# Three rounded-operand products in place of each float32 product in the second mixer of a two-layer kernel

## The reference

```python
proj = jnp.einsum('bsd,df->bsf', h, w_in)
q_a, k_a, v_a, z_a, q_r, k_r, v_r, z_r = jnp.split(proj, IN_SPLIT_IDX, axis=-1)
# 8 heads of 128: scores q_a k_a^T with three dilated windows and a slope for distance, softmax, times v_a
y_a = dilated_attention_mixture(q_a, k_a, v_a)
# 4 retention heads: (q_r k_r^T * decay) v_r in both directions, q_r and k_r of 128, v_r of 256, then a norm
y_r = bidirectional_retention(q_r, k_r, v_r, dec_f, dec_b)
y = jnp.concatenate([y_a * jax.nn.silu(z_a), y_r * jax.nn.silu(z_r)], axis=-1)
out = jnp.einsum('bsf,fd->bsd', y, w_out)
```

## Time and profile before

| | |
|---|---|
| time of the runs | 1528.95 us median of 3 (1528.47 to 1529.10) |
| time of the profiled execution | 1529.12 us |
| its span between first and last instruction | 1527.5 us |
| granted PE clock, mean | 0.998 |
| PE busy | 1513.2 us, 99% |
| DVE busy | 1138.6 us, 75% |
| ACT busy | 780.2 us, 51% |

### The profile page before, as it was taken

How to read it: one execution, slowest core, us unless ns; L and a number is a source line. 1 busy time by engine, 2 the same in 40 slices (tenths; PEclk the granted TensorE clock), 3 DMA queues, 4 the chain that set the end, 5 groups by cost and what they waited for, 6 DMA issues and landing times. The chain is left out here.

```text
span 1527.5 us, 32035 instructions
## 1 busy us (share of the span) xinstructions
PE 1513.2 (99%) x12546; PEld 1475.2 (97%) x12546; DVE 1138.6 (75%) x1389; ACT 780.2 (51%) x936; POOL 35.8 (2%) x61
## 2 busy tenths in 40 slices
PE   9999999999999999999999999999999999999997
PEld 8999997999999999999999999999999989999997
DVE  7878777668998878788788887879874644764754
ACT  7645456545454444444444444445654644454544
POOL 0000000000000000000000000000100000000000
PEclk9999999999999999999999999999999999999999
DMA  9574556557887867677676776866475554445451
GB/s 343 179 274 161 201 195 204 194 176 262 306 300 237 294 230 275 247 248 275 236 286 236 259 274 220 302 220 220 159 255 193 194 193 161 159 163 179 163 182 56
DMA packets 86428, 340.29 MB, mean 223 GB/s; under 512 B 9784, under 2 KB 10320, under 8 KB 79824
## 3 DMA queue, kind: packets, MB, share of 16 engines
q1 hardware_dynamic: 77904, 281.05, 53.1%
q0 software_dynamic: 7584, 55.61, 10.4%
q10 hardware_dynamic: 864, 2.53, 0.5%
HBM read 337.02 MB, written 2.13 MB: 222 GB/s over the span
## 5 line engine op out<-in xcount | busy, mean ns | idle before, releaser
L742 DVE TENSOR_TENSOR wlo<-raw,whi 128x1024 fp32r<-128x1024 f32 x528 | 642.6, 1222 | 332.2 <-ACT whi L359 328.4
L359 ACT ACTIVATE whi<-raw 128x1024 fp32r<-128x1024 f32 x527 | 556.6, 1060 | 631.8 <-PE PS L1421 561.8
L1417 PE MATMUL PS<-gh,whi 128*128 128x256 f32 x3048 | 846.1, 278 | 1.2 <-DVE wlo L742 0.9
L1421 PE MATMUL PS<-gh,wlo 128*128 128x256 f32 x3048 | 839.2, 275 | 0.0
L1419 PE MATMUL PS<-gl,whi 128*128 128x256 f32 x3048 | 839.1, 275 | 0.0
L1417 PEld LDWEIGHTS PS<-gh,whi 128*128 128x128 f32 x3048 | 572.2, 188 | 6.0 <-DVE wlo L742 2.7
L1419 PEld LDWEIGHTS PS<-gl,whi 128*128 128x128 f32 x3048 | 572.3, 188 | 0.8
L1421 PEld LDWEIGHTS PS<-gh,wlo 128*128 128x128 f32 x3048 | 572.1, 188 | 0.0
L1417 PE MATMUL PS<-ah,whi 128*128 128x256 f32 x688 | 189.2, 275 | 0.0
L1421 PE MATMUL PS<-ah,wlo 128*128 128x256 f32 x688 | 189.2, 275 | 0.0
L1419 PE MATMUL PS<-al,whi 128*128 128x256 f32 x688 | 189.2, 275 | 0.0
(11 more groups left out here) (272 smaller groups left out, 939.6 us busy)
## 6 DMA issues: line engine op xcount, KB each, us to landing
raw<-weights SPq DMA_DIRECT2D x527, 512.0 KB, 3.8
ada_w<-w_ada POOLq DMA_DIRECT2D x48, 1024.0 KB, 6.9
EM<-rows POOLq DMA_DIRECT2D x1, 3072.0 KB, 13.4
X<-xT SPq DMA_DIRECT2D x3, 512.0 KB, 8.7
c<-const ACTq DMA_DIRECT2D x1, 1536.0 KB, 6.9
c_act<-c_rows POOLq DMA_DIRECT2D x1, 1024.0 KB, 6.7
KF<-rows POOLq DMA_DIRECT2D x2, 512.0 KB, 6.1
outT<-X SPq DMA_DIRECT2D x2, 512.0 KB, 3.2
```

The lines of the kernel that those rows point to most:

```text
L359: act.activation(whi[:, j % SPLIT, first:first + 1024], raw[:, j, :], ACT.Copy).then_inc(s_hi, 1)
L742: dve.tensor_tensor(wlo[:, j % SPLIT, first:first + 1024], raw[:, j, :], whi[:, j % SPLIT, first:first + 1024].bitcast(F32), ALU.subtract) ...
L1417: pe.matmul(out[:, t, :], whi[:, b, w], hi[:, kt, :], start=first and half == 0 and (apart or t % 2 == 0), stop=False, skip_group_check=True)
L1421: mm = pe.matmul(out[:, t, :], wlo[:, b, w], hi[:, kt, :], start=False, stop=last and half == 1, skip_group_check=True)
```

## The change

Queries, keys, values, probabilities and decayed retention scores of the second mixer also get a high and a low part, and each of their float32 matmuls becomes three matmuls on `fp32r` parts (`split_product`). The low parts lie in tiles of `QB` that are idle at that time (table `LOW`), `QBR` being the same memory seen as `fp32r`.

The tiles:

```diff
+        QBR, _ = place("QBR", [P, 56, S], F32R, offset=ada_at)
+        LOW = {QR2: V02, KR2: V12, VR2: Q12, VR2 + 4: K12, Q02: QR2, K02: KR2, V02: VR2, Q12: Q02, K12: K02, V12: V02}
+        PTH2, _ = place("PTH2", [P, 2, 2, S], F32R, offset=o_pts)
+        PTL2 = QBR[:, VR2 + 4:VR2 + 8, :].rearrange("p (h c) s -> p h c s", h=2)
+        RETH, RETL = QBR[:, K02:K02 + 2, :], QBR[:, K02 + 2:K02 + 4, :]
```

ACT, in attention step 4, in retention step 0 and at the end of a group:

```diff
-                        act.activation(PTS[:, h % 2, :, :], PS[:, 5, :].rearrange("p (c d) -> p c d", c=2),
-                                       ACT.Copy).then_inc(s_pts, 1)
+                        act.activation(PTH2[:, h % 2, :, :], PS[:, 5, :].rearrange("p (c d) -> p c d", c=2),
+                                       ACT.Copy).then_inc(s_pth, 1)
...
+                    if step == 0:
+                        act.wait_ge(s_rs, r + 1)
+                        if r:
+                            act.wait_ge(s_ro, r)
+                        act.activation(RETH, SB2[:, r % 2, :, :], ACT.Copy).then_inc(s_rh, 1)
...
-                    act.activation(QB[:, 4 * g:4 * g + 4, :], acc_tiles((G_IN2 + g) % 2), ACT.Copy).then_inc(s_evac, 1)
+                    if 4 * g in LOW:
+                        act.activation(QBR[:, 4 * g:4 * g + 4, :], acc_tiles((G_IN2 + g) % 2), ACT.Copy).then_inc(s_qh, 1)
+                    else:
+                        act.activation(QB[:, 4 * g:4 * g + 4, :], acc_tiles((G_IN2 + g) % 2), ACT.Copy).then_inc(s_evac, 1)
```

DVE, in attention step 4, in `decayed` and two new functions, and where they are called in the slots:

```diff
+                if step == 4 and layer:
+                    dve.wait_ge(s_pth, h + 1)
+                    dve.tensor_tensor(PTL2[:, h % 2, :, :], PS[:, 5, :].rearrange("p (c d) -> p c d", c=2),
+                                      PTH2[:, h % 2, :, :].bitcast(F32), ALU.subtract).then_inc(s_pts, 1)
...
-                                         SCALE, DM[:, r, :, :], ALU.mult, ALU.mult).then_inc(s_rm, 1)
+                                         SCALE, DM[:, r, :, :], ALU.mult, ALU.mult).then_inc(s_rs, 1)
+
+            def decayed_low(r):
+
+                dve.wait_ge(s_rh, r + 1)
+                dve.tensor_tensor(RETL, SB2[:, r % 2, :, :], RETH.bitcast(F32), ALU.subtract).then_inc(s_rm, 1)
+
+            def low_part(g):
+
+                dve.wait_ge(s_qh, g - 3)
+                low = LOW[4 * g]
+                dve.tensor_tensor(QBR[:, low:low + 4, :], acc_tiles((G_IN2 + g) % 2),
+                                  QBR[:, 4 * g:4 * g + 4, :].bitcast(F32), ALU.subtract).then_inc(s_evac, 1)
...
+                    if step == 1:
+                        decayed_low(r)
...
+                if n % 8 == 7 and 4 * (n // 8) in LOW:
+                    low_part(n // 8)
                 slot2(n)
```

PE:

```diff
+            def split_product(out, left, left_low, right, right_low, first, last):
+
+                pe.matmul(out, left, right, start=first, stop=False, skip_group_check=True)
+                pe.matmul(out, left, right_low, start=False, stop=False, skip_group_check=True)
+                return pe.matmul(out, left_low, right, start=False, stop=last, skip_group_check=True)
...
-                            mm = pe.matmul(PS[:, 5, S * c:S * c + S], QB[:, KR2 + r, P * c:P * c + P], QB[:, QR2 + r, :],
-                                           start=True, stop=True)
+                            mm = split_product(PS[:, 5, S * c:S * c + S], *(QBR[:, k + r, P * c:P * c + P] for k in (KR2, LOW[KR2])),
+                                               *(QBR[:, k + r, :] for k in (QR2, LOW[QR2])), True, True)
...
-                                mm = pe.matmul(PS[:, 6, S * e:S * e + S], v,
-                                               SB2[:, r % 2, c, :], start=(c == 0), stop=(c == 1))
+                                mm = split_product(PS[:, 6, S * e:S * e + S], v, v_low, RETH[:, c, :], RETL[:, c, :], c == 0,
+                                                   c == 1)
```

More of the change, by code:

```diff
@@ L180, in build @@
         SB2, o = place("SB2", [P, 2, 2, S], offset=o)
+        o_pts = o
         PTS2, o = place("PTS2", [P, 2, 2, S], offset=o)
@@ L276, in build @@
         s_early, s_early_hi = sem("s_early"), sem("s_early_hi")
+        s_qh, s_pth, s_rs, s_rh = sem("s_qh"), sem("s_pth"), sem("s_rs"), sem("s_rh")
         s_copy, s_pool = sem("s_copy"), sem("s_pool")
@@ L1604, in attention @@
                 if layer:
-                    q, k = (QB[:, head_tile(*at_, h), :] for at_ in ((Q02, Q12), (K02, K12)))
-                    v = values(QB, V02 if h < 4 else V12, P)
+                    q, k = (tuple(QBR[:, tile + h % 4, :] for tile in (at_, LOW[at_]))
+                            for at_ in ((Q02, K02) if h < 4 else (Q12, K12)))
+                    v = tuple(values(QBR, tile, P) for tile in ((V02, LOW[V02]) if h < 4 else (V12, LOW[V12])))
                 else:
@@ L1638, in scores @@
                     at, keys = (S * c, S) if layer else (P * c, P + P * c)
-                    mm = pe.matmul(PS[:, 4, at:at + keys], q[:, P * c:P * c + P], k[:, 0:keys], start=True, stop=True)
+                    if layer:
+                        mm = split_product(PS[:, 4, at:at + keys], *(x[:, P * c:P * c + P] for x in q), *k, True, True)
+                    else:
+                        mm = pe.matmul(PS[:, 4, at:at + keys], q[:, P * c:P * c + P], k[:, 0:keys], start=True, stop=True)
                     if c == 1:
@@ L1659, in weighted @@
                     first = 0 if layer else P * b
-                    mm = pe.matmul(PS[:, 6, first:S], v(b, P * (h % 4)), PTS[:, h % 2, b, 0:S - first],
-                                   start=(b == 1), stop=(b == 0), skip_group_check=True)
+                    if layer:
+                        mm = split_product(PS[:, 6, 0:S], *(x(b, P * (h % 4)) for x in v), PTH2[:, h % 2, b, :],
+                                           PTL2[:, h % 2, b, :], b == 1, b == 0)
+                    else:
+                        mm = pe.matmul(PS[:, 6, first:S], v(b, P * (h % 4)), PTS[:, h % 2, b, 0:S - first],
+                                       start=(b == 1), stop=(b == 0), skip_group_check=True)
                     if b == 0:
@@ L1814, in slot2 @@
                             for c in range(2):
-                                v = values(QB, VR2 + 4 * (r // 2), P)(c, S * (r % 2) + P * e)
-                                mm = pe.matmul(PS[:, 6, S * e:S * e + S], v,
-                                               SB2[:, r % 2, c, :], start=(c == 0), stop=(c == 1))
+                                v, v_low = (values(QBR, k, P)(c, S * (r % 2) + P * e)
+                                            for k in (VR2 + 4 * (r // 2), LOW[VR2 + 4 * (r // 2)]))
+                                mm = split_product(PS[:, 6, S * e:S * e + S], v, v_low, RETH[:, c, :], RETL[:, c, :], c == 0,
+                                                   c == 1)
                         mm.then_inc(s_ro, 1)
```

## The result

The changed kernel takes 1535.86 us (median of 6 runs, 1534.97 to 1536.17), the kernel before 1528.87 (6 runs beside them, 1528.46 to 1529.22). The ratio is 1.0045, with a 95% interval of 1.0033 to 1.0058: it is slower by 7 us, on the side that was forecast, 3.7 us above the forecast and 0.14 us inside the upper end of the range. The profiled execution took 1536.02 us with a span of 1534.4; the span of before was 1527.5. So 6.9 us of span are to be found.

What follows compares the result with a forecast made beforehand. PE, busy for 99% of the span, was taken to set the time. Saving -5.7, tiles +0.3, waits +1.05, +2.2 and +4.7, restarts +0.5 gave +3.1 us on 1529.12: 1532.2 us, range 1529.3 to 1536.

Steps and rivals of the forecast that it cites:

- the five waits: PE waits for DVE's low parts in slots 63, 66, 68, 70 and 72: 1.05, 2.2 for three, and 4.7 us.
- PE sets the time: From 1265 to 1460 us PE is always busy; matmul time removed is won, waits added are lost; DVE's amount costs nothing.
- Group 7, slot 63: Head 0's score waits for group 7's low part, queued on DVE behind slot 63's split: 1.05 us.
- Slots 66, 68, 70: In retention PE waits for the decayed scores' low part behind the odd slot's split: 0.5, 0.85, 0.85 us.
- Slot 72: PE waits 4.7 us for head 3's low part, behind head 0's root and reciprocal, ACT's copy and slot 71's split.
- The rival of a short wait: Slot 72 waits 2.0 us instead of 4.7, sum +0.4, 1529.5 us; chance 14%.
- Attention has no wait: In attention, two microseconds of slack hide the copy and low part; uncovered, up to 1.3 us per head, 10 in all.
- The saving of a split product: 56 float32 matmuls of 0.44 us become three of 0.1133 each: 5.7 us saved, less 0.3 for tiles; mark 0.113 to 0.118.
- Restarts: A matmul after a wait can't hide its 0.188 us weight load; five waits cost 0 to 0.9, taken as 0.5 us.
- The clock stays up behind slot 72: Granted clock stays 1.00 behind slot 72; the rival, a fall costing 1.7 us, 1533.9 us, had 20%.
- slow tiles: Rival: matmuls on the new tiles take 0.125 instead of 0.115 us, adding 1.7, 1533.9 us; chance 10%.
- hidden low parts: Rival: PE finds every low part ready, only -5.4 us is left, 1523.7 us; chance 6%.

Runs made afterwards that it cites:

- all_moved: Changed kernel with next head's scores waiting only for bank 5, decayed scores and their low parts earlier on DVE, group 7's copy and low part before slot 63's split: 1524.73 us.
- scores_free: Changed kernel with PE's scores of the next head waiting for DVE's read of bank 5, not for the previous head's low part: 1533.57 us.
- low_early: Changed kernel with the low part of the decayed scores ahead of DVE's split in slots 65, 67, 69 and 71: 1527.08 us.
- decay_first: Changed kernel with the decayed scores ahead of DVE's other retention work in slots 64, 66, 68 and 70: 1531.96 us.
- padded: `all_moved` with 48 bytes between neighbouring groups of tiles from group 4 on: 1524.53 us.
- filled: Changed kernel with 36 matmuls of unused result on PE before the wait for head 3 in slot 72: 1533.29 us.
- attention_only: Changed kernel with split products in attention alone, retention keeping its 24 float32 matmuls: 1527.5 us, ratio 0.9991 to the kernel before.

## Why the prediction was right in its direction and too low in its size

The forecast was +3.1 us, the span shows +6.9. The measured time misses the stretch that had 50% (1531 to 1534) and lies in the range by 0.14 us, just short of the worst sum of waits, clock and tiles that the range left out; that it lies inside is luck. That the kernel is slower is not: the five waits that outweigh the saving are those that were named. Each step against what was measured:

- **PE sets the time.** Right. With the waits gone (`all_moved`) PE's shorter work is the whole gain; the 18 us of new DVE work cost nothing by their amount.
- **How a wait is counted.** The forecast counts from the moment at which the next matmul was due, one step of 0.113 behind the start of the last one. The profile's idle time begins only at the modelled end of that row, 0.28 behind its start, and so is 0.17 shorter for each wait. From start to start the five waits are 1.05, 0.62, 0.94, 0.95 and 4.61 us, 8.2 in all for 7.33 in the profile's rows and for 7.95 in the forecast.
- **Group 7, slot 63.** Forecast 1.05 us, measured 0.88 in the rows, once, and 1.05 from the start that was due. Right, though the forecast's own figures (PE there at 1270.87, the low part done at 1271.86) give 0.99.
- **Slots 66, 68, 70.** Forecast 0.5, 0.85 and 0.85, measured 0.45, 0.78 and 0.78. Right, and `scores_free` and `low_early` show that they are due to the low part behind the split.
- **Slot 72.** Forecast 4.7, measured 4.44, by the chain that was written down. Right, link by link: counted from head 3's score (1295.73), the decayed scores start at 7.1 us (forecast 6.90), ACT's split ends at 9.4 (9.25), the low part ends at 12.7 (12.6), and PE would have gone on at 8.2 (7.9). `low_early` and `decay_first` cut the chain at its last and its first link and leave 0.9 and 2.1. The rival of a short wait is out.
- **Attention has no wait.** Right: PE's window is full and no row of the waits names it.
- **The saving of a split product: mis-sized.** Forecast 5.4 us for 56, 0.10 each less 0.3. Measured in the attention slots and behind them: 2.4 us for 32, 0.074 each; at that, 1.8 for retention's 24, and 4.2 in all. `all_moved` confirms the sum, with 4.16 in PE's timeline and 4.2 in the medians. The new matmuls start 0.118 apart, the upper end of the step that the text gave as its mark; three of them are 0.354, and the float32 one they replace was worth 0.43 and not 0.44: four stand between 1294.32 and 1296.05 in the trace of before, 0.4325 each. The 0.44 was a remainder, 182.53 less products, transposes and sums, with the products at 0.113 per matmul throughout; but the stream runs at 0.118 for a while behind such an insertion (14 steps behind head 0's score, see `padded`). The Trainium skill's page "TensorE: Matmul & The Clock Gate", section "Wait — 56ns, not 53.3ns?", would have 0.109 for a matmul and made this term still larger; the trace has 0.118.
- **Restarts.** Forecast 0.5 for five waits. Retention lost 9.0 us of PE's time; less the waits by the profile's rows (7.33) and the clock (2.2), and with 1.8 of saving to be made up, 1.25 is left, 0.25 for each wait. Of these, 0.17 are the difference between the profile's idle time and the distance from start to start. What is left of the restarts is 0.4, near the forecast. The timeline shows it: the first matmul after a wait starts 0.22 or 0.19 before the second and not 0.118 (1271.43 to 1271.65, 1278.36 to 1278.55). The steps of 0.12 in the stream behind it belong to no wait, since the kernel before has them too (0.118 behind head 0's score).

```profile
1294.32 1.89 PE L1816 MATMUL PS<-SB,QB 128*128 128x256 f32 x8
```

(The kernel before; the next start, 1296.05, is in the earlier trace rows.)

- **The clock stays up behind slot 72: wrong, and the largest error.** It was a rival with 20%, priced at 1.7 us by the start of the kernel, and by the sign that the prediction named, a window below 1.00 behind slot 72, that rival was right. `filled` shows it: 2.2 us in the stretch, 2.6 between the medians. The sentence against it, that PE is dense on both sides, did not hold: PE was as dense on both sides in `filled`, and the granted clock fell with 4.44 us of idleness between and not with 0.19. The Trainium skill's page "TensorE: Matmul & The Clock Gate", section "What's actually happening", says that the lower level is the default and that activity releases the higher one. This case's trace agrees: 0.50 behind the idle stretch, 1.00 with `filled`'s matmuls in it.
- **The tail.** Not in the sum. In the profiled run the work behind the last product met the lower clock earlier and took 0.8 us more. That is probably not the change's: of the profiled runs of the variants, `filled`, `low_early`, `attention_only` and `padded` have a granted clock of 0.77 to 0.81 in the window from 10 to 5 us before the end, as before (0.76), and `scores_free`, `decay_first` and `all_moved` 0.56 to 0.59, like the changed kernel (0.55). Between `padded` and `all_moved`, which differ in the addresses of tiles alone, the spans are 1.1 us apart and the medians 0.2. Each kernel has one profile, so no trace shows one kernel on both courses. The mean clock on record with every run makes it likely: of the 43 runs of the kernel before beside the experiments, 25 have 0.998 and a median of 1528.7, and 18 have 0.997 and a median of 1529.2.

The rivals: slow tiles would have been 0.125 apart and were 0.118; hidden low parts are what `all_moved` makes of them, and a gain of 4.2 us, not 5.4, was in it.

By the measured terms: -4.2 for the products, +8.2 waits from start to start, +0.4 restarts, +2.2 clock, +0.8 tail, -0.5 start = +6.9. The waits were forecast within 0.3 and the restarts within 0.1. Of the 3.8 us that the forecast lacked, 2.2 are the clock behind the long wait and 1.2 the saving that was set too high; the rest is in waits, tail and start.

## What to carry to other kernels

Where one engine is busy all the time, price a new operation by the place of its instruction in the queue of the engine that does it, not by that engine's idle time: the 18 us of low parts here cost 0 or 11 us. What made the difference was whether five of them, four decayed scores and a group's copy stand ahead of other work or behind it, and which semaphore the next head's scores wait for. Read a wait of TensorE from start to start: the profile's idle time was 0.17 us shorter than what each wait took, and the first step behind it cost 0.07 to 0.1 more. A wait of several microseconds has a second price behind it: with 4.44 us of idleness the profiled executions lost 1.6 to 2.2 us more to the lower clock, and with 2.11 us 1.6 in the one that is traced, one of three such runs in eleven. So a chain that makes one long wait is to be broken first. Where a float32 matmul is replaced by three on parts, the gain is thin (0.074 of 0.43 us here), and it takes the whole absence of such waits to see it.

## What the runs showed of the hardware that was not expected

- With 2.11 us of idleness of TensorE the granted clock was still 1.00 when it resumed, fell 0.7 to 0.8 us later in the middle of dense matmuls (the window 1307 to 1308 at 0.69), and did so, by the times and the mean clocks, in three runs of eleven. With 4.44 us it was down already before TensorE resumed in the changed kernel, and back 4.8 us after the first matmul; in `scores_free`, with a wait of the same length, it fell only 0.9 us after TensorE had resumed and was back 3.3 us after the fall (0.66 in the window 1307 to 1308, 0.63 from 1310 to 1311). So the length of the wait alone didn't decide the course. Waits of 0.45 to 0.9 us never moved it.
- A matmul of 256 columns has two steady distances at a granted clock of 1.00, 0.113 us in the undisturbed stream and 0.118 in the new matmuls. The second isn't bound to their tiles: the stream's own matmuls have it too for 0.8 to 1.7 us behind other work (7 in 0.82 us from 1271.08 in `all_moved`, 14 in 1.65 us from 1271.85 in the kernel before, whose scores are float32). 48 bytes more between the groups of tiles changed nothing (`padded`).
- At the end of the kernel the granted clock took one of two courses in the nine profiled executions (0.76 to 0.81 in five, 0.55 to 0.59 in four), with about 0.8 us between them and no tie to the edits that is known. Spans of single profiled executions can't be compared more closely than that here.
